# The feed-forward part of a transformer block on one core: low parts of the split operands moved from Pool to VectorE, and gated forms stored as high and low parts

## The reference

```python
def swiglu(xn, w_gate, w_up, w_down):
    return (jax.nn.silu(xn @ w_gate) * (xn @ w_up)) @ w_down
...
    h = h + swiglu(rmsnorm(h, norm_ffn[i]), f_w_gate[i], f_w_up[i], f_w_down[i])
return rmsnorm(h, norm_final)
```

## Time and profile before

| | us |
|---|---|
| median of 3 runs (1488.72 to 1490.7) | 1490.35 |
| the profiled execution: its own time | 1491.57 |
| the profiled execution: span of its instructions | 1489.3 |
| PE busy in it | 1404.8 (94%) |
| DVE, ACT, Pool busy | 897.6 (60%), 480.0 (32%), 610.8 (41%) |
| mean granted clock of TensorE | 0.985 |
| strips 0 to 19 | from 817.4 to 1228.8 |
| down passes 0 to 19 | from 1228.8 to 1451.3 |

### The profile page before, as it was taken

The page is one execution under the profiler, slowest core; times in us unless marked ns, Lnnn a source line. Parts: engine busy times, 40 slices in busy tenths (PEclk is TensorE's granted clock), DMA queues, the critical chain, the costliest instruction groups (busy, mean ns, idle before and its releaser), DMA issues.

```text
span 1489.3 us, 17800 instructions
## 1 busy us (share of the span) xinstructions
PE 1404.8 (94%) x6801; PEld 1162.8 (78%) x6801; DVE 897.6 (60%) x1441; ACT 480.0 (32%) x822; POOL 610.8 (41%) x414
## 2 busy tenths in 40 slices
PE   7999999999989899999889799999999988989897
PEld 6989889889877787777668588878888866767677
DVE  6547456466566823343677854455554448888875
ACT  6223313223334431222244333333333243323222
POOL 5313322313334321121144744444444456776761
PEclk9999999999999999999999899999999999999999
DMA  5201110201412210001130232233332255334312
GB/s 171 57 29 57 29 57 30 57 29 32 125 57 86 86 57 29 29 29 57 55 137 21 92 104 85 101 107 106 106 103 86 95 191 198 127 127 129 109 61 113
DMA packets 91844, 124.95 MB, mean 84 GB/s; under 512 B 4912, under 2 KB 66416, under 8 KB 91248
## 3 DMA queue, kind: packets, MB, share of 16 engines
q1 hardware_dynamic: 91760, 123.82, 25.1%
HBM read 97.06 MB, written 26.74 MB: 83 GB/s over the span
## 4 chain that ended last, share of the span: by engine, by line
PE 71%; DVE 17%; issue 7%; ACT 2%; POOL 1%; SPq 1%; DMA 1%; DVEq 0%; POOLq 0%; ACTq 0%
PE PS L1767 12%; PE PS L1769 12%; PE PS L1768 12%; PE PS L2088 6%; PE PS L2090 6%; PE PS L2089 6%; PE PS L2116 2%; PE PS L2118 2%; PE PS L2117 2%; PE PS L1970 2%; PE PS L1995 2%; DVE T2T L1632 2%; DVE raw L1633 2%; DVE xT L1651 2%; PE PS L1909 1%
## 5 line engine op out<-in xcount | busy, mean ns | idle before, releaser
L708 POOL TENSOR_TENSOR WL<-raw,WH 128x1024 fp32r<-128x1024 f32 x52 | 126.7, 2449 | 319.8 <-ACT WH L857 319.8
L1767 PE MATMUL PS<-XH,WH 128*128 128x512 f32 (+1 forms) x448 | 177.8, 397 | 4.1 <-POOL WL L708 2.4
L1769 PE MATMUL PS<-XH,WL 128*128 128x512 f32 (+1 forms) x448 | 169.3, 378 | 0.0
L1768 PE MATMUL PS<-XL,WH 128*128 128x512 f32 (+1 forms) x448 | 169.1, 378 | 0.0
L1465 DVE TENSOR_TENSOR xT<-PS,xT 128x512 f32<-128x512 f32 x128 | 88.1, 691 | 68.4 <-PE PS L1769 66.9
L1767 PE MATMUL PS<-YH,WH 128*128 128x512 f32 x256 | 104.8, 409 | 1.8 <-issue 1.8
L1769 PE MATMUL PS<-YH,WL 128*128 128x512 f32 x256 | 101.1, 395 | 0.0
L1767 PEld LDWEIGHTS PS<-XH,WH 128*128 128x128 f32 x448 | 85.4, 191 | 19.9 <-issue 5.2
L1768 PE MATMUL PS<-YL,WH 128*128 128x512 f32 x256 | 100.4, 392 | 0.0
L1602 DVE TENSOR_TENSOR U<-PS,U 128x512 f32<-128x512 f32 x50 | 33.6, 689 | 108.3 <-PE PS L2090 106.3
L1769 PEld LDWEIGHTS PS<-XH,WL 128*128 128x128 f32 x448 | 85.3, 190 | 16.0
(11 more groups left out here) (401 smaller groups left out, 3792.0 us busy)
## 6 DMA issues: line engine op xcount, KB each, us to landing
raw<-in_f_w_up_dram SPq DMA_DIRECT2D x11, 1024.0 KB, 5.3
rawE<-in_f_w_gate_dram SPq DMA_DIRECT2D x10, 1024.0 KB, 5.5
forms<-U SPq DMA_DIRECT2D x40, 256.0 KB, 2.0
raw<-in_f_w_down_dram SPq DMA_DIRECT2D x40, 256.0 KB, 3.6
raw<-in_a_w_in_dram SPq DMA_DIRECT2D x8, 1024.0 KB, 5.3
acc<-forms SPq DMA_DIRECT2D x12, 512.0 KB, 4.3
forms<-STG SPq DMA_DIRECT2D x20, 256.0 KB, 2.1
RYB<-forms SPq DMA_DIRECT2D x10, 512.0 KB, 4.1
```

The costliest lines, as they stand in the source:

```text
L708: last = gp.tensor_tensor(WL[:, n % 2, at], raw_of(n)[:, at], WH[:, n % 2, at].bitcast(F32), ALU.subtract)
L1767: mm(dst, wh, xh, start=(k == 0), stop=False)
L1768: mm(dst, wh, xl, start=False, stop=False)
L1769: last = mm(dst, wl, xh, start=False, stop=(k == len(tiles) - 1))
```

## The change

Of the low parts of the gate and up weights, two of five groups (m = 0 and 4, after groups 3 and 4 changed places) stay on Pool for strips 1 to 19, each in two halves of 128x512; the others, all five of strip 0 and those of the combined x go to DVE. The chunks take pieces 1 to 10 and piece 0 becomes the one left for the end, so its four quarters are stored as they are (`ud`) and no forms are made in strip 0. Pieces 1 and 2 (chunk 0) are stored as plain forms and split when loaded, all on DVE. The forms of pieces 3 to 9 are split during their strips, those of piece 10 during passes 1 to 9: high part by ACT into one of three staging buffers `HS`, low part by DVE in place, both stored; in the passes of chunk c both parts of the forms of chunk c + 1 are loaded straight into the cells, so no form is split there. In DVE's queue the form operations move behind the first sum, and all weight combinations of a pass go ahead of its adds. The first loads for chunk 0 and the down weights are reordered on SP.

```diff
+    W_POOL = (0, 4)
+    PLAIN = 2
+    FORM_ORDER = (0, 5, 1, 6, 2, 3, 4)
+    SUM_AT, SPLIT_AT = (1, 2), 3
...
+        first_forms = xform[2:7] + [xform[2], raw[:, 1024:].rearrange("p (u s) -> p u s", u=2)]
...
+            def store_form(j, f):
+                n = split_count(j, f)
+                sp.wait_ge(s_yhi, n)
+                sp.dma_start(yhd[j - 1 - PLAIN, f], HS[n % 3][:, :].bitcast(F32)).then_inc(s_hst[n % 3], 16)
+                sp.wait_ge(s_ylo, n)
+                sp.dma_start(yld[j - 1 - PLAIN, f], yforms(j)[f]).then_inc(s_yst[f], 16)
...
+                if s == NS - 1:
+                    load_down(0)
+                    load_first(6)
+                    sp.wait_ge(s_pp, PROD * (NS - 1))
+                    for f in range(5):
+                        load_first(f)
+                    sp.dma_start(xT[:, 0:2, :], xd[:, 0:2, :]).then_inc(s_xr[0], 16)
...
+            sp.wait_ge(s_fl, 1)
+            load_first(5)
+            sp.wait_ge(s_fl, 5)
+            sp.dma_start(xT[:, 4:6, :], xd[:, 4:6, :]).then_inc(s_xr[2], 16)
+            sp.wait_ge(s_fl, 6)
+            sp.dma_start(xT[:, 2:4, :], xd[:, 2:4, :]).then_inc(s_xr[1], 16)
+            sp.wait_ge(s_fl, 7)
+            load_down(1)
...
             for s in range(1, NS):
-                for m in range(5):
+                for m in W_POOL:
                     block_lo(s, m)
```

In ACT's queue for the strips (`j = s // 2`, `late = s % 2`):

```diff
-                if not more:
-                    down_hi(0)
                 copy_out(s, 0)
...
+                else:
+                    for m in range(3):
+                        down_hi(0, m)
+                    form_hi(0)
+                    form_hi(1)
                 copy_out(s, 1)
+                if j > PLAIN:
+                    for f in FORM_ORDER[4 * late:4 + 4 * late]:
+                        split_form_hi(j, f)
...
+                if s + 1 == NS:
+                    for f in range(2, 6):
+                        form_hi(f)
                 copy_out(s, 2)
+            form_hi(6)
+            down_hi(1, 0)
```

In DVE's queue for the strips:

```diff
-                    combine_y(s // 2)
                 if s + 1 < NS:
                     combine_w(s + 1)
...
                 sum_out(s, 0)
...
+                if s + 1 < NS:
+                    block_lo(s + 1, 1)
+                    block_lo(s + 1, 2)
+                else:
+                    form_lo(0)
+                    form_lo(1)
+                if j and not late:
+                    for i in range(4):
+                        combine_y(j, i)
+                if j > PLAIN:
+                    split_form_lo(j, FORM_ORDER[4 * late])
                 sum_out(s, 1)
+                if s + 1 < NS:
+                    block_lo(s + 1, 3)
                 sum_out(s, 2)
...
+                if j > PLAIN:
+                    for f in FORM_ORDER[4 * late + 1:4 + 4 * late]:
+                        split_form_lo(j, f)
+            for f in range(2, 6):
+                form_lo(f)
             sum_out(NS - 1, 3)
             sum_out(NS - 1, 4)
+            form_lo(6)
```

In DVE's queue for the passes:

```diff
-                add_down(g, 0)
                 if g + 1 < NC * NP2:
                     combine_down(g + 1, 0)
-                add_down(g, 1)
-                add_down(g, 2)
-                if g + 1 < NC * NP2:
                     combine_down(g + 1, 1)
...
+                for i in range(6):
+                    add_down(g, i)
+                if g in SUM_AT:
+                    for i in range(2):
+                        combine_y(NJ - 1, 2 * SUM_AT.index(g) + i)
+                if SPLIT_AT <= g < SPLIT_AT + 7:
+                    split_form_lo(NJ - 1, FORM_ORDER[g - SPLIT_AT])
                 add_down(g, 6)
```

More of the change, by code:

```diff
@@ L46, in build_block @@
     NF = len(STRIPS)
-    STRIPS += [("gate", 0), ("up", 0), ("last", NJ - 1)]
+    STRIPS += [("gate", 0), ("up", 0), ("last", 0)]
     AT = {s: n for n, s in enumerate(STRIPS)}
@@ L325, in cell, with split_count, block_lo_ready, blocks_lo_ready @@
             return hi[:, at:at + 2, :], lo[:, at:at + 2, :]
-        def form_src(c, f):
-            if c == 0:
-                return first_forms[f]
-            return form_ring[(7 * (c - 1) + f) % 3]
-        def form_lo_count(c, f):
-            mine = [i for i in range(7) if (i in FORM_DVE) == (f in FORM_DVE)]
-            return len(mine) * c + mine.index(f) + 1
+        def split_count(j, f):
+            return 7 * (j - 1 - PLAIN) + FORM_ORDER.index(f) + 1
+        def block_lo_ready(eng, s, m):
+            if s > 0 and m in W_POOL:
+                eng.wait_ge(s_blp, 4 * (s - 1) + 2 * W_POOL.index(m) + 2)
+            else:
+                mine = [i for i in range(5) if i not in W_POOL]
+                eng.wait_ge(s_bld, m + 1 if s == 0 else 5 + len(mine) * (s - 1) + mine.index(m) + 1)
+        def blocks_lo_ready(eng, s):
+            block_lo_ready(eng, s, 4)
+            if s:
+                block_lo_ready(eng, s, 3)
         s_const = sem("s_const")
@@ L430, in build_block @@
         s_sf = sem("s_sf")
-        s_yst = sem("s_yst")
+        s_ust = sem("s_ust")
+        s_ul = sem("s_ul")
+        s_yhi = sem("s_yhi")
+        s_ylo = sem("s_ylo")
+        s_hst = [sem(f"s_hst{i}") for i in range(3)]
+        s_yst = [sem(f"s_yst{i}") for i in range(7)]
         s_rx = [sem(f"s_rx{i}") for i in range(7)]
-        s_ry = [sem(f"s_ry{i}") for i in range(3)]
+        s_cell = [[sem(f"s_cell{c}{i}") for i in range(7)] for c in range(2)]
         s_xr = [sem(f"s_xr{i}") for i in range(4)]
@@ L439, in build_block @@
         s_fh = sem("s_fh")
[L440 to L441 removed]
+        s_fl = sem("s_fl")
         s_p2 = sem("s_p2")
@@ new lines, in _ @@
+                j, late = s // 2, s % 2
+                if j and j <= PLAIN and not late:
+                    for f in (0, 1, 5, 2, 6, 3, 4):
+                        store_plain(j, f)
+                if j > PLAIN:
+                    for f in FORM_ORDER[4 * late:4 + 4 * late]:
+                        store_form(j, f)
+            sp.wait_ge(s_fl, 1)
[3 more added lines that the diff above has]
+            sp.wait_ge(s_fl, 6)
@@ L1164, in _ @@
             form_x_hi(0)
+            block_hi(0, 1)
+            block_hi(0, 2)
             silu_first(2)
             silu_first(3)
+            block_hi(0, 3)
+            block_hi(0, 4)
             form_x_hi(2)
-            for m in range(1, 5):
-                block_hi(0, m)
             form_x_hi(3)
+            form_x_hi(1)
             for s in range(NS):
-                more = s + 1 < NS
-                if s % 2:
+                j, late = s // 2, s % 2
+                if late:
                     silu(s - 1, 2)
@@ L1187, in _ @@
                 copy_out(s, 1)
-                if more:
-                    block_hi(s + 1, 2)
-                    block_hi(s + 1, 3)
-                else:
-                    for f in range(4, 7):
-                        form_hi(0, f)
-                if s % 2 == 0:
+                if j > PLAIN:
+                    for f in FORM_ORDER[4 * late:4 + 4 * late]:
+                        split_form_hi(j, f)
+                if not late:
                     silu(s, 0)
+                    silu(s, 1)
@@ L1599, in sum_out @@
                     dve.wait_ge(s_cp, 3 * s + (1, 2, 0, 3)[i])
+                if i == 1 and s % 2 and s > 1:
+                    dve.wait_ge(s_yst[1], 16 * (s // 2))
                 if i == 2:
@@ L1671, in _ @@
             pieces(5, range(6, KT))
-            for i in range(4):
+            combine_x(0)
+            combine_w(0)
+            for i in range(1, 4):
                 combine_x(i)
-            combine_w(0)
+            for m in range(5):
+                block_lo(0, m)
             form_x_lo(0, 0)
@@ L1677, in _ @@
             up_evac(3)
+            form_x_lo(2, 2)
+            form_x_lo(3, 4)
             for s in range(NS):
+                j, late = s // 2, s % 2
                 if s:
```

340 lines of the change are left out of this document (147 added, 193 removed).

## The result

The changed kernel took 1454.7 us (median of 4 runs, 1453.08 to 1455.57) against 1489.53 for the kernel before in the same session (1487.86 to 1490.7): a ratio of 0.9766, with a 95% interval from 0.9749 to 0.9783. The forecast was 1450 with a range of 1441 to 1464. The profiled execution took 1454.84 us, its span 1452.9, which is 36.4 less than before; the forecast for the span was 40.6 less.

The account below looks back on a forecast made before the run. TensorE was taken as the bound, busy 94% of the span, with about 57 us of idle time and slow clock to win. The terms -7.6 - 10.1 - 6.2 + 7.3 - 24.0 = -40.6 gave 1450 us, range 1441 to 1464.

Parts of the forecast that it names:

- Nothing ahead of strip 0: The change touches only the feed-forward phase, from 817.4 us to 1451.3 us, so nothing earlier moves.
- A: Even strips: with form operations behind the first sum no wait is left; -7.6 us over nine strips.
- rival 2: Even strips: DVE becomes the bound, block 6's 0.5 us margin is exceeded, 1457 to 1464 us; chance 18%.
- B: Strip 0: four gate forms leave DVE, low parts join it, the strip becomes 22.5 us; -10.1 us.
- C: Strip 19: ACT copies X before starting on the down weights, so its 4.4 us wait goes; -6.2 us.
- D: Down pass 0 gets worse: late form 5 and a shared buffer delay weight 1, wait 10.5 us; +7.3 us.
- E: Down passes 1 to 19: no forms split from chunk 1 on, combinations first with Pool idle; -24.0 us.
- Rival 1: Shifted low parts win nothing because Pool and DVE are one resource; A and B vanish, 1468 us; chance 5%.
- rival 3: Down pass 0 hardly waits, form 5 being early; D is +1.5 and the time 1444 us; chance 10%.
- Rival 4: Form loads bound the down passes, making the kernel slower, 1567 us at 139 GB/s; chance 4%.
- Rival 5: Down passes: the changed order does nothing because the adds are the limit; E stays, 1474 us; chance 3%.

Follow-up runs that it names:

- x1: Changed kernel with Pool making the low part of piece 0's up weights before the norm statistics again; the median falls by 2.3 us.
- x6: Changed kernel with the four form operations ahead of the weight combinations again, low parts left as changed; even strips stay at 19.22 us.
- x7: Changed kernel with all seven low parts of a strip's weights on Pool again, DVE's order left as changed; 1454.9 us.
- x2: Changed kernel with seven own buffers for the first forms, loaded at strip 19's start, and down weight 1 requested right behind; 1449.8 us.
- x3: x2 with DVE's queue reordered where strip 19 meets pass 0 and form 6's low part on Pool; 1447.8 us.
- x4: Changed kernel with Pool making the last weights' low parts in pass 18, not pass 17; the median falls by 1.8 us.
- x8: Changed kernel with both even-strip parts undone: form operations ahead of weight combinations, all seven weight low parts on Pool; 1461.22 us.
- x5: Changed kernel with the down passes' weight combinations in pairs behind the first and third add again; passes 1 to 17 keep 9.55 to 10.0 us.
- x9: Changed kernel with x1, x2, x3 and x4 together, weight 2 loaded early and later combinations between the adds; 2.7 us above its expected 1438.
- x12: x9 with all seven weight low parts on Pool and the last gate's two products moved behind pass 1's third add; 1439.37 us.

## Why the prediction was right, and where not

The time lay in the range, the sign and the mechanisms were those forecast, and the likeliest value was 4.7 us too low. By its steps:

- **Nothing ahead of strip 0** is the step that failed. The forecast let the change touch only the feed-forward phase. The order of two calls on Pool before it was in the change too, and it costs 2.3 us (x1; 2.4 by the starts of strip 0 in thirteen profiles). Each queue that a step moves past has to be read, outside the phase as well; the earlier trace rows start at 817.4.
- **A, -7.6**: measured -7.5. The margin that was given for block 6, 0.5 us, was too small; it is 1.9 in strip 10. Four Pool halves were counted at 1.3 each. The first lies beside a sum that reads PSUM, and three DVE operations are held up, by 1.1 each. x6 takes 4.3 of the 4.6 to spare before block 4 (its first sum ends 10.6 into strip 10) without harm, x7 takes none of either margin (6.3 and 14.4), and rival 2 never came. What the forecast did not see is that the new order alone is enough here (x7).
- **B, -10.1**: measured -11.8. The wait of 2.0 before block 4 came out at 0.2. DVE's chain up to the first sum takes 28.2 (802.4 to 830.6) and not 30.1: Pool holds up one of its operations, by 1.0 (1.67 for 0.69), where two halves of 1.3 had been counted. That the sum ended so near the forecast 830.4 is luck, since chain and strip both began 2.1 late; in x1 it ends at 827.8, again 11.1 into the strip. The wait before block 6 was forecast at 1.2 and is 1.2. No run tells the forms that left strip 0 from the low parts that moved.
- **C, -6.2**: measured -6.1, with no wait. The trace alone shows it; no run put ACT's copy back behind the weight.
- **D, +7.3**, was mis-sized: +8.9. The wait was 11.4 for 10.5, and the clock took 2.3 for 1.6: eleven matmuls were 0.43 to 0.56 apart and not 0.23. The chain was right link by link: `raw` free 27.6 after the start of strip 19 (forecast 27.1), weight 1 landed at 31.5 (31.2), the add done at 34.6 (33.8), where Pool held the last combination for a whole 1.37 and not for part of it. That both halves of the chain are real is shown by x2 (5.0 gone with the shared place) and x3 (the rest gone with DVE's order and form 6's low part on Pool).
- **E, -24.0**: measured -22.0. Of the 2.0 that lack, 1.3 is pass 18, where Pool's low parts of the last weight meet DVE's first combination; these operations were in the profile before and nothing was said of them. x4 takes it away. The rest is in the passes on W2A, which take 9.8 and not the 9.64 assumed (last section).
- **Rival 1** is ruled out as priced, for A and B did not vanish, and x8 against x6 shows a gain from the moved low parts. But in the order that the change has they win nothing, as the rival says (x7); **rival 3** by the trace. **Rival 4** had been given a bound of 193 GB/s; in passes 1 to 19 the loads moved 227 GB/s at a DMA share of 0.67 and nobody waited. **Rival 5** is ruled out by E itself. x5 adds that the place of the combinations, which the forecast counted on beside the splits that are gone, is not needed. That the splits alone won the passes is what is left over. The first combination, 517 ns and not 1562, fits it, but no run put the splits back, so the largest term has its cause from the trace and not from a run.

## What to carry to other kernels

When work is taken off a busy pair of engines, cost its queue from both ends: list what stands ahead of the one operation that the bound engine waits for, and when that operation is due, since parts that seem separate (a reordering and an offload) may each be enough alone and together be paid for once. Compare the issue order of every engine over the whole program, not only in the phase that the change is about: a swap of two calls cost 2.3 us here. And when a long wait goes, look at the queues that hid behind it, SP's first; it took three further edits (x3, x9, x12) before the 11.4 us of pass 0 were not paid again in pass 1 or 2.
